# Six of eleven down chunks in the seven-product form, in groups of three turns

## The reference

```
x = x + 0.5 * swiglu(rms(x))
swiglu(h) = (silu(h @ w_gate) * (h @ w_up)) @ w_down     # 1024 -> 2816 -> 1024
```

## Time and profile before

| | us |
|---|---|
| median of 3 runs | 1182.74 (1182.23 to 1182.81) |
| the profiled execution | 1182.64 |
| its span in the profile | 1180.7 |
| TensorE busy | 1173.8 |
| VectorE busy | 944.4 |
| ScalarE busy | 688.1 |
| granted TensorE clock, mean | 0.999 |

### The profile page before, as it was taken

How to read it: one execution, slowest core, us unless ns; L and a number is a source line. 1 busy time by engine, 2 the same in 40 slices (tenths; PEclk the granted TensorE clock), 3 DMA queues, 4 the chain that set the end, 5 groups by cost and what they waited for, 6 DMA issues and landing times.

```text
span 1180.7 us, 17445 instructions
## 1 busy us (share of the span) xinstructions
PE 1173.8 (99%) x6787; PEld 1025.7 (87%) x6787; DVE 944.4 (80%) x1102; ACT 688.1 (58%) x925; POOL 105.0 (9%) x97
## 2 busy tenths in 40 slices
PE   9999999999999999999999999999999999999998
PEld 8888889889989888888888888889887898888886
DVE  6687897875657689888978988997887676798887
ACT  7566556853557566555565655564576556565553
POOL 1010001420142010000010000010012121000000
PEclk9999999999999999999999999999999999999999
DMA  9966755454344465665655656547623435666561
GB/s 319 334 205 197 204 188 179 144 182 141 141 145 176 143 197 162 212 212 181 202 189 177 208 185 205 185 143 214 212 92 127 144 114 166 203 217 198 191 195 55
DMA packets 164013, 214.93 MB, mean 182 GB/s; under 512 B 14832, under 2 KB 139120, under 8 KB 163824
## 3 DMA queue, kind: packets, MB, share of 16 engines
q1 hardware_dynamic: 163664, 213.30, 56.2%
q0 software_dynamic: 144, 0.52, 0.1%
q10 hardware_dynamic: 144, 0.26, 0.1%
HBM read 213.02 MB, written 1.05 MB: 181 GB/s over the span
## 4 chain that ended last, share of the span: by engine, by line
PE 98%; DMA 1%; ACT 0%; POOL 0%; DVE 0%; SPq 0%; issue 0%; POOLq 0%; DVEq 0%
PE ps L2302 30%; PE ps L2309 16%; PE ps L2281 15%; PE ps L2282 15%; PE ps L2283 15%; PE ps L2385 1%; PE ps L2572 1%; PE ps L3036 1%; PE ps L2892 1%; DMA arena<-in_first 1%; PE ps L3059 0%; PE ps L2580 0%; PE ps L2997 0%; PE ps L2994 0%; PE ps L2453 0%; PE ps L2644 0%
## 5 line engine op out<-in xcount | busy, mean ns | idle before, releaser
L2302 PE MATMUL ps<-hT,w_parts 128*128 128x512 f32 x1568 | 375.4, 391 | 0.3 <-issue 0.2
L2302 PEld LDWEIGHTS ps<-hT,w_parts 128*128 128x128 f32 x1568 | 289.8, 188 | 59.6 <-issue 1.5
L1355 DVE TENSOR_TENSOR w_parts<-raw,w_parts 128x2048 fp32r<-128x2048 f32 x85 | 196.2, 2317 | 58.0 <-ACT w_parts L749 57.9
L2309 PEld LDWEIGHTS ps<-hT,w_parts 128*128 128x128 f32 x1568 | 201.4, 191 | 8.0 <-DVE w_parts L1431 0.2
L884 ACT ACTIVATE w_parts<-raw 128x2048 fp32r<-128x2048 f32 x108 | 206.1, 1908 | 0.6 <-DMA raw<-in_ffn_w_gate 0.6
L749 ACT ACTIVATE w_parts<-raw 128x2048 fp32r<-128x2048 f32 x85 | 162.4, 1920 | 73.5 <-PE ps L2283 70.5
L2309 PE MATMUL ps<-hT,w_parts 128*128 128x256 f32 x1568 | 204.1, 283 | 0.0
L1571 DVE TENSOR_TENSOR w_parts<-raw,w_parts 128x2048 fp32r<-128x2048 f32 x45 | 103.0, 2289 | 14.3 <-ACT w_parts L884 14.3
L2281 PE MATMUL ps<-w_parts,arena_r 128*128 128x512 f32 (+1 forms) x264 | 102.8, 389 | 0.0
L2282 PE MATMUL ps<-w_parts,arena_r 128*128 128x512 f32 (+1 forms) x264 | 102.8, 389 | 0.0
L2283 PE MATMUL ps<-w_parts,arena_r 128*128 128x512 f32 (+1 forms) x264 | 102.3, 387 | 0.0
(11 more groups left out here) (373 smaller groups left out, 1975.1 us busy)
## 6 DMA issues: line engine op xcount, KB each, us to landing
raw<-in_ffn_w_down SPq DMA_DIRECT2D x44, 1024.0 KB, 5.0
raw<-in_ffn_w_gate SPq DMA_DIRECT2D x43, 1024.0 KB, 5.4
raw<-in_ffn_w_up SPq DMA_DIRECT2D x43, 1024.0 KB, 5.4
raw<-in_xattn_wkv SPq DMA_DIRECT2D x16, 1024.0 KB, 5.4
raw<-in_even_w_in SPq DMA_DIRECT2D x13, 1024.0 KB, 5.2
raw<-in_xattn_wq SPq DMA_DIRECT2D x8, 1024.0 KB, 5.1
raw<-in_xattn_wo SPq DMA_DIRECT2D x8, 1024.0 KB, 5.4
raw<-in_odd_w_in SPq DMA_DIRECT2D x6, 1024.0 KB, 5.6
```

The source lines that it names most:

```text
L1355: ins = V.tensor_tensor(lo, src, hi.bitcast(F32), ALU.subtract)
L2302: mm(ps[:, bank0 + m, :], cols(w_hi, n, k, CW, m * P, (m + 1) * P), hT[:, k, :, :].rearrange("p a c -> p (a c)"), start=k == 0, stop=False)
L2309: last = mm(ps[:, bank0 + m, SEQ:], cols(w_lo, n, k, CW, m * P, (m + 1) * P), hT[:, k, 0, :], start=False, stop=k == KT - 1)
```

## The change

Each later stage uses the form for six down chunks, the first stage for four. In the later stages the three pairs of turns 4 to 9 become two groups of three turns: `turn_mixed`, `turn_mixed_next`, `turn_read`. Two forms stand in a row in a group. ScalarE copies the results of the first one out into a second store, `Mixed.fresh`, and VectorE adds `fresh` to `kept` at the end of the reading turn, in two additions of [128 x 1024], counted by the semaphore `fresh_added`. Before its last turn VectorE waits for the second group's additions. In the first stage the additional form belongs to hidden block 2: VectorE runs `turn_mixed_next` in turn 2, TensorE multiplies it in turn 3, ScalarE copies its results out in turn 3, and the result of turn 5, which ScalarE copied before, is now added by VectorE.

```diff
--- before.py
+++ after.py
@@ -443,13 +443,14 @@
         kept_later = [xn[:, t, :].rearrange("p (q c) -> p q c", c=512) for t in range(TT)]
 
         class Mixed:
-            FIRST, COUNT = (2, 0, 0, 0), (3, 5, 5, 5)
+            FIRST, COUNT = (1, 0, 0, 0), (4, 6, 6, 6)
             w_sums = part(3072, [3, 512])
             gu_sums = part(4608, [3, P])
             w_hi, w_lo = (mixed_parts[:, 1536 * i:1536 * (i + 1)].rearrange("p (a c) -> p a c", c=512) for i in range(2))
             gu_hi, gu_lo = (mixed_parts[:, 3072 + 384 * i:3072 + 384 * (i + 1)].rearrange("p (a c) -> p a c", c=P)
                             for i in range(2))
-            kept = [[part(at_, [2, 512]) for at_ in (10240, 4992)], kept_later, kept_later, kept_later]
+            fresh = [part(at_, [2, 512]) for at_ in (10240, 4992)]
+            kept = [fresh, kept_later, kept_later, kept_later]
 
         class Even:
             xpad = part(0, [XT, SEQ + 3])
@@ -509,13 +510,19 @@
         mixed_mm = [halves_hi] + [es["dec_mm"]] * 3
         mixed_read = [quarter_in[0]] + [es["kz_done"]] * 3
 
+        fresh_added = es["dx_done"]
+
+        def fresh_added_at(f, g):
+
+            return (g - 1) * 2 + (1 + (f - 1) * 4)
+
         def mixed_end(f):
 
             return Mixed.FIRST[f] + Mixed.COUNT[f]
 
         def counted(f, i, each, first, extra=0):
 
-            return (i - Mixed.FIRST[f]) * each + (1 + (f - 1) * (5 * each + extra) if f else first)
+            return (i - Mixed.FIRST[f]) * each + (1 + (f - 1) * (6 * each + extra) if f else first)
 
         def w_sums_at(f, i):
             return counted(f, i, 4, 4)
@@ -876,7 +883,7 @@
                     nc.scalar.activation(dst, gu.rearrange("p (k c) -> p k c", k=2),
                                          ACT.Copy).then_inc(gu_hi_done, 1)
 
-                def turn(j, between=lambda c: None, mixed=None, first_out=None):
+                def turn(j, between=lambda c: None, mixed=None, first_out=None, group=None):
 
                     def split(m):
                         act.wait_ge(raw_in[m % RING], (j - 1) * 16 + landed(m))
@@ -897,15 +904,18 @@
                     if mixed is not None and first_out is None:
                         sums_hi()
                     if first_out is not None:
+                        out_to = Mixed.kept[f] if group is None else Mixed.fresh
                         act.wait_ge(mixed_mm[f], mixed_mm_at(f, first_out) + 1)
-                        nc.scalar.activation(Mixed.kept[f][0], ps[:, 0:2, :], ACT.Copy).then_inc(mixed_read[f], 1)
+                        if group is not None:
+                            act.wait_ge(fresh_added, fresh_added_at(f, group))
+                        nc.scalar.activation(out_to[0], ps[:, 0:2, :], ACT.Copy).then_inc(mixed_read[f], 1)
                     act.wait_ge(chunks_used, j * 3 + (base + 2))
                     if mixed is not None:
                         act.wait_ge(gu_summed[f], gu_sums_at(f, mixed) + 4)
                         nc.scalar.activation(Mixed.gu_hi, Mixed.gu_sums, ACT.Copy)
                     hidden(j + (f * FJ + 1), gu_hi)
                     if first_out is not None:
-                        nc.scalar.activation(Mixed.kept[f][1], ps[:, 2:4, :], ACT.Copy).then_inc(mixed_read[f], 1)
+                        nc.scalar.activation(out_to[1], ps[:, 2:4, :], ACT.Copy).then_inc(mixed_read[f], 1)
                     if mixed is not None and first_out is not None:
                         sums_hi()
                     split(base + 4 + RING)
@@ -939,11 +949,11 @@
                 if f == 0:
 
                     turn(1)
-                    turn(2)
-                    turn(3, lambda c: mem_hi(range(3 * c, min(3 * c + 3, KT))))
+                    turn(2, mixed=1)
+                    turn(3, lambda c: mem_hi(range(3 * c, min(3 * c + 3, KT))), first_out=1)
                     turn(4, lambda c: c and squares(1, mem_rows, lambda t, h: act.wait_ge(mem_in, 16), tiles=(c - 1,)),
                          mixed=2)
-                    turn(5, first_out=2)
+                    turn(5)
                     turn(6, mixed=3)
                     turn(7)
                     turn(8, mixed=4)
@@ -952,9 +962,10 @@
                     turn(1, mixed=0)
                     turn(2, mixed=1, first_out=0)
                     turn(3)
-                    with act.Fori(2, mixed_end(f)) as i:
-                        turn(i * 2, mixed=i)
-                        turn(i * 2 + 1)
+                    with act.Fori(1, 3) as g:
+                        turn(g * 3 + 1, mixed=g * 2)
+                        turn(g * 3 + 2, mixed=g * 2 + 1, first_out=g * 2, group=g)
+                        turn(g * 3 + 3)
                 made[0] = base + FFN_CHUNKS - 1
                 gate_out(FJ - 1, base + FFN_CHUNKS - 3)
                 hi_upto(base + FFN_CHUNKS)
@@ -1624,7 +1635,7 @@
                     V.tensor_tensor(Mixed.w_lo, Mixed.w_sums, Mixed.w_hi.bitcast(F32), ALU.subtract)
                     split(m)
 
-                def turn_read(j, i):
+                def turn_read(j, i, group=None):
 
                     def split(m):
                         dve.wait_ge(hi_done, (j - 1) * 3 + (m + 1))
@@ -1637,11 +1648,18 @@
                     up_sum(j)
                     product(j)
                     dve.wait_ge(mixed_read[f], mixed_read_at(f, i))
+                    if group is not None:
+                        dve.wait_ge(fresh_added, fresh_added_at(f, group))
                     mixed_out(i, 0, None)
                     split(base + 3 + RING)
                     mixed_out(i, 1, j * 3 + (base + 2))
                     hidden_lo(j, gu_hi, gu_lo)
                     split(base + 4 + RING)
+                    if group is not None:
+                        dve.wait_ge(mixed_read[f], mixed_read_at(f, i) + 2)
+                        for half in range(2):
+                            V.tensor_tensor(Mixed.kept[f][half], Mixed.kept[f][half], Mixed.fresh[half], ALU.add)\
+                             .then_inc(fresh_added, 1)
 
                 def turn(j, between=lambda c: None):
 
@@ -1689,10 +1707,10 @@
                     hidden_lo(0, gu_hi, gu_lo)
                 if f == 0:
                     turn(1)
-                    turn(2)
+                    turn_mixed_next(2, 1)
                     turn(3, lambda c: mem_lo(range(3 * c, min(3 * c + 3, KT))))
                     turn_mixed(4, 2)
-                    turn(5)
+                    turn_read(5, 2)
                     turn_mixed(6, 3)
                     turn_read(7, 3)
                     turn_mixed(8, 4)
@@ -1702,10 +1720,13 @@
                     turn_mixed(1, 0)
                     turn_mixed_next(2, 1)
                     turn_read(3, 1)
-                    with dve.Fori(2, mixed_end(f)) as i:
-                        turn_mixed(i * 2, i)
-                        turn_read(i * 2 + 1, i)
+                    with dve.Fori(1, 3) as g:
+                        turn_mixed(g * 3 + 1, g * 2)
+                        turn_mixed_next(g * 3 + 2, g * 2 + 1)
+                        turn_read(g * 3 + 3, g * 2 + 1, group=g)
                 made[0] = base + FFN_CHUNKS - 1
+                if f:
+                    dve.wait_ge(fresh_added, fresh_added_at(f, 3))
                 kept_sum(0, 2, 0)
                 kept_sum(1, 3, 2)
                 gate_sum(FJ - 1)
@@ -2544,14 +2565,20 @@
 
                 turn(1, True)
                 if f == 0:
-                    with pe.Fori(2, 4) as j:
-                        turn(j, False)
+                    turn(2, False)
+                    turn(3, False, mixed=1)
                 else:
                     turn(2, False, mixed=0)
                     turn(3, False, kept=1, mixed=1)
-                with pe.Fori(2, mixed_end(f)) as i:
-                    turn(i * 2, False, kept=i)
-                    turn(i * 2 + 1, False, mixed=i)
+                if f:
+                    with pe.Fori(1, 3) as g:
+                        turn(g * 3 + 1, False, kept=g * 2)
+                        turn(g * 3 + 2, False, mixed=g * 2)
+                        turn(g * 3 + 3, False, kept=g * 2 + 1, mixed=g * 2 + 1)
+                else:
+                    with pe.Fori(2, mixed_end(f)) as i:
+                        turn(i * 2, False, kept=i)
+                        turn(i * 2 + 1, False, mixed=i)
                 turn(FJ - 1, False, held=f == 3, kept=mixed_end(f))
                 n = base + FFN_CHUNKS - 1
                 pe.wait_ge(lo_done, n + 1)

```

## The result

The changed kernel takes 1188.03 us (median of 5 runs, 1187.69 to 1190.3) against 1182.81 (5 runs, 1182.23 to 1183.81): ratio 1.0052, 95% interval 1.004 to 1.0063. It is slower by 5.2 us; the forecast was 1189.1, with a range of its own from 1187.5 to 1190.5 and a wider one from 1185.5 to 1191.5. Two of the five executions took 1190.21 and 1190.3, at a mean granted clock of 0.997; the other three had 0.999 or 1.0. The profiled execution took 1188.0, with a span of 1186.2 (before 1180.7) and a granted clock of 0.999.

What follows compares the result with a forecast made beforehand. TensorE, busy 99% of the span, was taken as the bound, with VectorE possibly late for it. Terms -2.7 + 2.45 + 2.0 + 2.0 + 2.7 = +6.4 us on 1182.64 gave 1189.1; own range 1187.5 to 1190.5, wider 1185.5 to 1191.5.

Steps and rivals of the forecast that it cites:

- 12 products saved, 0.68 us a form: TensorE, one further seven-product down chunk in each of four stages: 0.68 us saved each, -2.7 us.
- Inside the groups nothing: Later stages' groups of three turns: TensorE waits for nothing, though VectorE has 48.4 us of work against 48.35.
- The rival with 0.13: Waits inside the groups if VectorE is 0.5 us slower a turn: six of 0.4 us, +2.4, 1191.5; chance 0.13.
- The release, 0.36 us throughout: Time from the end of VectorE's instruction to TensorE's next matmul, read behind `mixed_out` in a later stage: 0.36 us.
- `kept_sum` 7.75 us into turn 10: Later stages' last turn: VectorE starts `kept_sum` 7.75 us into TensorE's turn 10, 2.87 later than before.
- The ends of the second and third stage, 2.0 us each: `hidden_lo` comes 2.8 us later against a margin of 0.8, so TensorE waits 2.0 us in each stage.
- The fourth stage, 2.7: End of the fourth stage: with a margin of 0.06 us, TensorE waits 2.7 us for `hidden_lo`.
- The first stage, +1.8 net: ScalarE's queue delays its copy, TensorE starts turn 4 at 70.05; 2.45 us lost, net +1.8.
- about 3.2: First stage, upper end of the cost: about 3.2 us if VectorE's up read behind `mem_lo` delays the last two products.
- The clock: Rival: TensorE at 1.2 GHz after four pauses, 5.4 us more per closing chunk, about +22, 1211; chance 0.02.
- the prediction's first rival: Additions hidden: VectorE less than 0.8 us later into turn 10, first stage in time, only -2.7 remains: 1180.0; chance 0.08.

Runs made afterwards that it cites:

- run 9: Kernel before with the fourth form in the first stage only, and turn 3's memory parts put behind what TensorE needs: 1181.95 us, ratio 0.9995.
- run 10: Changed kernel without the additions of the first group of three turns in each later stage; those ahead of the last turn stay: 1189.44 us, ratio 1.0053.
- run 2: Changed kernel with the first stage as before, so only the three later stages changed: 1188.15 us, ratio 1.0042.
- run 4: Changed kernel with two more [128 x 1024] additions on VectorE ahead of the last turn of each later stage: 1201.58 us, ratio 1.0158.
- run 5: Changed kernel with the first stage as before and the second store's additions on GpSimd instead of VectorE: 1204.22 us, ratio 1.0183.
- run 8: Changed kernel with the additions on GpSimd and the first stage's turn 3 memory parts put behind what TensorE needs: 1203.10 us, ratio 1.0174.
- run 6: Changed kernel with the later stages' last-turn `kept_added` (VectorE's additions to x) put behind `hidden_lo`: 1186.69 us, ratio 1.0035.

## Why the prediction was right, step by step

- **12 products saved, 0.68 us a form.** Shown by the count, and by run 9's turn 4 within 0.01 us.
- **Inside the groups nothing.** True in the profile of the change and by run 10. The rival with 0.13 occurs in some executions (run 2): the range should carry it as a spread and not as a case. With VectorE's work of 48.4 us against 48.35 there was nothing to take up a chunk that landed 0.9 or 2.4 us later.
- **The release, 0.36 us throughout.** It was read once, behind `mixed_out`, and taken for all. The waits in the traces show several: 0.05 us behind `gate_sum` and `up_sum`, 0.15 behind `hidden_lo`, 0.34 behind ScalarE's copy ahead of turn 4, 0.36 to 0.63 behind `mixed_out`.
- **`kept_sum` 7.75 us into turn 10.** Measured 7.67.
- **The ends of the second and third stage, 2.0 us each.** Measured 1.61. The mechanism was right, the size was off in one term, the release. I took 0.36 us; from `hidden_lo`'s end it took 594.10 - 593.95 = 0.15, and in the fourth stage 1173.34 - 1173.19 = 0.15. With it the sum would have said 1.8; the other 0.2 are VectorE's part, as `hidden_lo` began 2.62 us later against TensorE's turn 10 (17.34 against 14.72 us into it) where 2.8 were reckoned.
- **The fourth stage, 2.7.** Measured 2.31, by the same two terms.
- **The first stage, +1.8 net.** Measured 1.56; turn 4 at 69.85 instead of 70.05. One wait was not in the sum, for the up sum (L1523), which stood behind `mem_lo`: 0.95 us at 67.29. It cost nothing of its own, since ScalarE's copy came later still; it was the named bound of "about 3.2" that did not come.
- **The clock.** In the profile of the change it held. The rival had it fall in all four pauses, for 22 us. What occurs is milder: in the change's two runs at 0.997 some 2.2 us (1190.3 and 1190.21 against 1188.03), and in runs 2 and 10 the windows show the place, behind the last wait of the fourth stage. With waits of 3.7 to 4.4 us (run 4) it fell in all four runs (0.991 to 0.996).

The sum of the measured terms is -2.7 + 2.24 + 1.61 + 1.61 + 2.31 = +5.1, where +6.4 was forecast and 5.2 measured. All four losses were reckoned too large, by 1.4 us in all, so the match of the mechanism is better than that of the number. That the median lies within the narrow range is in part luck: three of the five executions kept their clock. In run 10, with the same waits, only two did, and its median is 1189.44; run 2's five executions spread over 4.7 us.

One figure of the prediction's first rival is off: for VectorE to be less than 0.8 us later into turn 10, its reading turn would have to end 2.0 us earlier than reckoned (2.8 - 0.8), not 1.6. The rival becomes less likely by it, and the sum doesn't use it.

## What to carry over

A saved matmul is worth its time only while the engine that pays for it has margin at the one instruction TensorE waits for next: ask where a new operation stands, not how busy its engine is on average. Here each addition of VectorE ahead of the last block of a stage came back in full, in the middle of the stage it cost nothing, and a queue of other work ahead of a single copy cost more than the products saved. Another order on the same engines took the two waits of the first stage away (run 9); moving the additions to GpSimd, while VectorE worked in SBUF, cost far more than it relieved. And a stretch reckoned to have no margin should be forecast as a spread, since one late chunk is enough to make it wait.

## What the runs showed of the hardware

- The granted clock fell, to 0.50 to 0.70 in windows of 3 us, behind five of the six waits of 1.9 us in run 5 and behind two of the same six in run 8; behind 2.1 us in run 2 (0.58); in the fourth stage behind 2.15 us in some executions (0.55 in run 10) and not in others (1.00 in the profile of the change); and not behind those of 1.45 us (1.00 from 594 to 597 in the profiles of the change and of run 10). So here a wait near 2 us can cost more than its length, 1.3 to 1.7 us more each time the clock fell (matmuls 0.43 us apart instead of 0.227, counted in the timelines of runs 2, 5, 8 and 10). The spread of the times goes with it: 2.6 us over the runs of the change, 0.3 in run 6, whose waits all stay at or under 1.5.
- An addition of [128 x 1024] by GpSimd takes 2.7 to 4.3 us (mean 3.3) beside VectorE, whose instruction in the meantime ends only behind it: 2.2 us lost each time, more than the 1.2 that the addition takes on VectorE.
- The time from the end of the instruction that TensorE waits for to its next matmul is not one number: 0.05 us behind `gate_sum` and `up_sum` (67.29 in the profile of the change, all six waits of run 5), 0.15 behind `hidden_lo`, which writes the operand, 0.34 behind ScalarE's copy ahead of turn 4 of the first stage (69.85), 0.13 behind another copy of its (710.25 in run 5), and 0.36 to 0.63 behind `mixed_out` (477.30 and 527.62 in run 2). Why they differ is not shown.
